# GpSimd splits each weight unit in six instructions instead of two

## The reference

```python
def first_block(x, ...):      # hybrid layer
    proj = rms_norm(x, norm_pre_w) @ w_in                 # 1024 -> 4104
    a = moba_attention(q, k, v) * silu(a_z)               # 8 heads of 64
    qkv = silu(causal_depthwise_conv(concat(d_q, d_k, d_v), conv_w))
    g = gated_delta_rule(qkv, g, beta)                    # 4 heads of 128
    mixed = concat(a, rms_norm(g) * silu(d_z)) @ w_out
    return x + rms_norm(mixed, norm_post_w)

def second_block(x, ...):
    proj = rmsnorm(h, norm1_g) @ w_in
    y_a = hgrn2_mixer(...)                                # 4 heads of 128
    y_b = nsa_mixer(...)              # compressed, selected and window attention
    merged = sigmoid(g_a) * (y_a @ w_br_a) + sigmoid(g_b) * (y_b @ w_br_b)
    h = h + merged @ w_out
    h = h + square(relu(rmsnorm(h, norm2_g) @ w_ff1)) @ w_ff2   # 1024 -> 4096 -> 1024
    return rmsnorm(h, final_g)
```

## Time and profile before

| | |
|---|---|
| median of 3 runs | 1343.54 us (1341.25 to 1349.25) |
| profiled execution | 1340.13 us, span 1338.1 us |
| TensorE busy | 1246.7 us, 93% |
| VectorE busy | 642.6 us, 48% |
| GpSimd busy | 580.2 us, 43% |
| ScalarE busy | 317.1 us, 24% |
| mean granted TensorE clock | 0.969 of full speed |

### The profile page before, as it was taken

How to read it: one execution, slowest core, us unless ns; L and a number is a source line. 1 busy time by engine, 2 the same in 40 slices (tenths; PEclk the granted TensorE clock), 3 DMA queues, 4 the chain that set the end, 5 groups by cost and what they waited for, 6 DMA issues and landing times.

```text
span 1338.1 us, 17644 instructions
## 1 busy us (share of the span) xinstructions
PE 1246.7 (93%) x6326; PEld 1034.9 (77%) x6326; DVE 642.6 (48%) x1189; ACT 317.1 (24%) x639; POOL 580.2 (43%) x332
## 2 busy tenths in 40 slices
PE   7898899998799799999997999998999999999996
PEld 6676688887688677788786888876888888888885
DVE  3974546548472478563735444457153500153202
ACT  3114221121472123311213344431031200021001
POOL 5543323322104456454420333334666666666662
PEclk9998999999899899999977999999999999999998
DMA  6211111100101222223420111112223232222321
GB/s 234 95 63 47 48 33 47 47 32 31 48 1 48 86 78 95 64 79 111 150 79 17 48 48 48 48 51 77 82 92 97 98 104 94 95 94 94 115 89 63
DMA packets 28870, 99.29 MB, mean 74 GB/s; under 512 B 3472, under 2 KB 5904, under 8 KB 28176
## 3 DMA queue, kind: packets, MB, share of 16 engines
q1 hardware_dynamic: 26592, 91.60, 20.7%
q10 hardware_dynamic: 2224, 6.94, 1.5%
HBM read 95.39 MB, written 2.10 MB: 73 GB/s over the span
## 4 chain that ended last, share of the span: by engine, by line
PE 55%; DVE 3%; issue 1%; ACT 0%; DVEq 0%; ACTq 0%
PE acc L266 15%; PE acc L268 15%; PE acc L267 15%; PE aux L449 3%; PE aux L467 2%; PE aux L716 2%; PE aux L457 1%; PE aux L745 0%; PE aux L641 0%; PE aux L328 0%; DVE mt_lo L1238 0%; DVE merged_b L1246 0%; PE aux L761 0%; DVE k_padded L1125 0%; DVE normalized L1288 0%
## 5 line engine op out<-in xcount | busy, mean ns | idle before, releaser
L1338 POOL CAST w_hi<-w_raw 128x1024 fp32r<-128x1024 f32 x164 | 175.0, 1067 | 724.7 <-issue 530.3
L1340 POOL TENSOR_TENSOR w_lo<-w_raw,w_hi 128x1024 fp32r<-128x1024 f32 x164 | 405.0, 2470 | 13.2
L266 PE MATMUL acc<-ht_hi,w_hi 128*128 128x512 f32 x672 | 283.5, 422 | 9.3 <-DVE feature_major L1588 5.1
L268 PE MATMUL acc<-ht_hi,w_lo 128*128 128x512 f32 x672 | 265.6, 395 | 0.0
L267 PE MATMUL acc<-ht_lo,w_hi 128*128 128x512 f32 x672 | 265.1, 394 | 0.0
L266 PEld LDWEIGHTS acc<-ht_hi,w_hi 128*128 128x128 f32 x672 | 128.9, 192 | 40.7 <-issue 8.9
L267 PEld LDWEIGHTS acc<-ht_lo,w_hi 128*128 128x128 f32 x672 | 128.9, 192 | 30.3 <-issue 4.3
L268 PEld LDWEIGHTS acc<-ht_hi,w_lo 128*128 128x128 f32 x672 | 128.0, 190 | 28.0
L266 PE MATMUL acc<-w_hi,ht_hi 128*128 128x512 f32 x256 | 106.4, 416 | 0.3 <-DVE feature_major L1009 0.3
L268 PE MATMUL acc<-w_hi,ht_lo 128*128 128x512 f32 x256 | 101.3, 396 | 0.0
L267 PE MATMUL acc<-w_lo,ht_hi 128*128 128x512 f32 x256 | 101.0, 395 | 0.0
(11 more groups left out here) (350 smaller groups left out, 1950.5 us busy)
## 6 DMA issues: line engine op xcount, KB each, us to landing
w_raw<-units SPq DMA_DIRECT2D x164, 512.0 KB, 3.3
cmp_w<-w_kv ACTq DMA_DIRECT2D x4, 1024.0 KB, 5.2
residual<-x SPq DMA_DIRECT2D x4, 512.0 KB, 6.9
result<-normalized SPq DMA_DIRECT2D x4, 512.0 KB, 2.8
consts_sb<-consts SPq DMA_DIRECT2D x1, 1344.5 KB, 11.4
norm_post_sb<-norm_post ACTq DMA_DIRECT2D x1, 512.0 KB, 4.7
cmp_tokens<-feature_major ACTq DMA_DIRECT2D x4, 128.0 KB, 2.9
final_sb<-final_g ACTq DMA_DIRECT2D x1, 512.0 KB, 3.3
```

The source lines that it names most:

```text
L266: nc.tensor.matmul(bank, ah, bh, start=start, stop=False)
L268: return nc.tensor.matmul(bank, al, bh, start=False, stop=stop)
L1338: nc.gpsimd.tensor_copy(w_hi[:, slot], raw[:, j]).then_inc(hi_split, 1)
L1340: nc.gpsimd.tensor_tensor(w_lo[:, slot], raw[:, j], w_hi[:, slot].bitcast(F32), ALU.subtract).then_inc(w_split, 1)
```

## The change

Each unit is split by six instructions instead of two. The cast becomes two of 128x512, one for each block of rows, and the subtraction four of 128x256, half a block each. The semaphores hi_split and w_split are raised once per unit, by the last of the two and of the four. The waits of all engines stay as they are.

```diff
                 slot = j % PARTS
-                nc.gpsimd.tensor_copy(w_hi[:, slot], raw[:, j]).then_inc(hi_split, 1)
+                for kk in range(2):
+                    done = nc.gpsimd.tensor_copy(w_hi[:, slot, kk], raw[:, j, kk])
+                done.then_inc(hi_split, 1)
                 pool.wait_ge(hi_split, unit + 1)
-                nc.gpsimd.tensor_tensor(w_lo[:, slot], raw[:, j], w_hi[:, slot].bitcast(F32),
-                                        ALU.subtract).then_inc(w_split, 1)
+                for kk in range(2):
+                    for first in (0, NC // 2):
+                        cols = slice(first, first + NC // 2)
+                        done = nc.gpsimd.tensor_tensor(w_lo[:, slot, kk, cols], raw[:, j, kk, cols],
+                                                       w_hi[:, slot, kk, cols].bitcast(F32), ALU.subtract)
+                done.then_inc(w_split, 1)
```

## The result

| | before | after |
|---|---|---|
| median | 1342.39 us (4 runs, 1338.27 to 1349.25) | 1322.19 us (4 runs, 1320.62 to 1329.17) |
| profiled execution, span | 1340.13, 1338.1 | 1321.77, 1320.0 |
| VectorE busy | 642.6 | 589.3 |
| GpSimd busy | 580.2 | 726.5 |
| mean granted clock | 0.969 | 0.980 |

The account below looks back on a forecast made before the run. TensorE was taken as the bound, stopped by any split over 4.76 us. Terms of 12 + 4.4 + 0.5 - 2 - 7.4 - 1.4 gave +6.1 us: 1346.2 profiled, about 1350 as median, range 1326 to 1370.

Parts of the forecast that it names:

- The bound and the cushion: TensorE bounds the kernel at 5.44 us per unit; a GpSimd split, then 3.51, has 1.25 spare, so 4.76 stops TensorE.
- The price of a seam: Each GpSimd unit: a lone split takes 3.9 us; a dense one, with VectorE entering at five seams, 6.15.
- the tiles: Delta-rule tiles: four TensorE waits of 1.85 us for gdn_U go, -7.4 us.
- the feed-forward: First product, eight slabs: a dense unit costs TensorE 1.4 us each, the unit before 0.1; together +12 us.
- the compressed keys: Units 70 to 72: the forecast said nothing of them; change put at 0.
- units 45 to 54: 495 to 538 us: dense units put TensorE 5.4 us back, against a shorter ScalarE wait and 1.7 of clock; +0.5 us.
- the convolution: 38 to 105 us: VectorE's 16 instructions finish at 58, but GpSimd falls behind; TensorE reaches the bank at 62.3; -2 us.
- the merge: 904 to 936 us: two waits on merged_b, 3.4 us, go; two tight units lose 1.0 each; -1.4 us.
- VectorE passes cheaply and the gains win: Rival, chance 0.18: a pass costs GpSimd only 0.33 us; -10 to -15 us, 1325 to 1333.
- GpSimd did not become the bound: Rival, with dense units much worse, 0.17: pieces cost over 0.3 us each beyond their share, tightly fed units lose; 1360 to 1380.
- the burst did not stay whole: Rival, chance 0.2: GpSimd's pieces follow directly, VectorE gets in nowhere new; 0 to +6 us, 1340 to 1350.
- The chains of tiny instructions: VectorE's rsqrt steps at 24, 476 and 655 us: six blocked about 0.6 each instead of two at 0.8 and 2.1; 0.

Follow-up runs that it names:

- tiles-only kernel: The kernel before, with six instructions only for units 16 to 31, the delta-rule tiles; 1330.44 us, ratio 0.9933.
- feed-forward-only kernel: The kernel before, with six instructions only for the feed-forward's 64 units (100 to 163), two for the first 100; 1354.97 us, ratio 1.007.
- casts-only kernel: The kernel before, with the cast in two of 128x512 and the subtraction whole in every unit; 1326.11 us, ratio 0.9868.
- keys-only experiment: The kernel before, with six instructions only for units 68 to 71, just ahead of the compressed keys; 1336.73 us, ratio 0.9981.

## Why the prediction was wrong

**The bound and the cushion** held. TensorE starts 0.05 us after the end of w_lo (976.87 to 976.92) where 0.13 had been allowed, so the limit was 4.84 and not 4.76.

**The price of a seam** was nearly right: a lone split 4.06 against 3.9, a dense one 6.24 against 6.15. VectorE does get in at seams without a semaphore; no VectorE instruction of the tiles or the feed-forward takes more than 1.23 us, so none is held longer than one piece. The feed-forward cost 10.5 against 12, the heads 2.7 against 4.4. (By the estimate in the prediction from the Trainium skill, GPSIMD Engine Reference, Performance versus the Vector engine, a fixed 0.29 us per instruction, the lone split would be 3.51 + 4 x 0.29 = 4.67, where the prediction wrote 4.5 to 4.6; the trace shows 4.06.)

**Where it failed is on the side of the gains**, and in one stall. Forecast and profiled change are 24.2 us apart (+6.1 and -18.1): 8.8 in the compressed keys, 4.0 in units 45 to 54, 3.3 in the convolution, 3.1 in the tiles, 1.7 in the heads, 1.6 in the merge and 1.5 in the feed-forward.

*Stalls that did not come.* The step said that two dense units at 1.3 and two at 1.4 put TensorE 5.4 back ahead of unit 52, and let that eat the 4.2 us wait. Units 45 to 50 changed by 0.7, 0.2, -0.3, -0.1, 0.4 and 0.1: 1.0 in all. To stall TensorE by 1.4, a unit needs five VectorE instructions ready one behind the other; I had taken that for four units from the way VectorE was held before. The splits of units 46, 47, 50 and 51 took 5.80, 5.68, 5.49 and 5.15 us, none 6.15, and before had lost 0.5 in unit 47 itself. Nor does the second of two such units in a row pay its excess over 4.84. The split of unit 47 began at 484.86, as soon as that of unit 46 was done, and TensorE needed 5.63 from unit to unit: it lost 0.19, the excess over its own 5.44. That is the mis-sized number. The rest of the step, a shorter wait and the clock kept, was right and unopposed: -4.6, and -3.5 for the stage where +0.5 had been written.

*The convolution* was given 1.2 us per VectorE instruction, 19 us for 16, and GpSimd behind at 62.3. It took 16.7 (38.80 to 55.48), 1.04 each, and TensorE reached the bank at 61.7. So TensorE gained 3.3 up to there, counted from its first unit, and not 2.3. The text names the full clock behind the wait, but prices it nowhere and lets the next three units take "it" back. It was 2.64 us (unit 8 took 8.49, then 5.85), and the units behind took back 0.6 and 0.9. Not all of it is the change's: in three of four kernels with before's program here unit 8 took 6.9 to 7.1. -5.3 against -2.

*The tiles* were credited with the wait for gdn_U alone, 1.85. The instructions behind it (L1668 of before) are caught less long too; 2.2 in each of the four stages up to unit 30 and 1.7 in the one behind. -10.5 against -7.4. *The merge* likewise, -3.0 against -1.4.

*The compressed keys* were put at nothing under the small chains. The profile of before had a wait of 2.98 us and 15.5 us at a clock of 0.54 there, more clock lost than anywhere else in the kernel, and no step of the prediction looked at it. Of the 18.1 us between the two spans, 8.8 come from here: 0.7 is the wait, 5.6 the clock of the 64 matmuls (13.00 against 7.36), and the rest lies in the matmuls around them. Some of the 8.8 is the scatter of single executions. Three of the four kernels with before's program in this stage took 3.2 to 3.3 less than before did, most of it because 32 matmuls a little further on (L745) took 3.79 to 4.61 us there and 6.42 in before. Against those three the changed kernel's stage is 5.5 shorter. Whether that rest is the change's doing stays open, as below; the ratio of 0.985 holds it in most executions.

Without the keys the stages add to about -9, so the sign would have been missed in any case, by the first three terms. The rival that ended on the right side ("VectorE passes cheaply and the gains win") had a wrong mechanism: a pass costs 0.44, not 0.33, and the feed-forward paid in full. What it had right was that the gains and the clock behind them outweigh the price. GpSimd did not become the bound, and the burst did not stay whole.

**The chains of tiny instructions** came out even, as said: six of them take 0.52 to 0.67 instead of two that take 0.96 and 2.25. But they show one way in which a whole subtraction can cost time in one execution and not in another. In before's profile the four instructions of L397 behind the chain are held little; in an execution of the tiles-only kernel, with whole splits at this place, one of them stood behind a subtraction, and TensorE waited 2.3 us longer:

```profile
481.01 1.91 DVE L397 TENSOR_SCALAR rstd_diagonal<-consts_sb,small 128x128 f32<-128x128 f32 x4
483.06 1.10 PE L359 MATMUL aux<-rstd_diagonal,consts_sb 128*128 128x512 f32 x2 [1.53 <-DVE rstd_diagonal L397]
```

```profile
470.58 4.23 DVE L397 TENSOR_SCALAR rstd_diagonal<-consts_sb,small 128x128 f32<-128x128 f32 x4
474.95 2.05 PE L359 MATMUL aux<-rstd_diagonal,consts_sb 128*128 128x512 f32 x2 [3.86 <-DVE rstd_diagonal L397]
```

The stage, units 34 to 45, then took 80.2 us instead of 75.7. The same happened in both places in the feed-forward-only kernel (37.7 against 33.2 at its start, units 0 to 5, and 80.3 here). In the profiles of the six kernels with split subtractions at these places the four instructions take 1.98 us at the most; that is seen, not proved, since it is one execution each. Nor does a whole subtraction make a kernel scatter by itself: the four executions of the casts-only kernel lie within 1.9 us.

## What to carry to other kernels

Where VectorE and GpSimd exclude each other, the length of one GpSimd instruction is the longest that VectorE can be made to wait, and each seam costs what it lets through: here 0.14 us for the piece and 0.44 for the pass. Cut the instructions where VectorE is on the path that TensorE waits for, and leave them whole where the fed engine has less slack than the dense split takes. The first cut, one more seam, brings most of the gain. When such a change is priced, count for a stalled unit only the instructions that are really ready, and for the second of two stalled units only what exceeds the fed engine's own time. Take the clock behind each wait into the sum: here it was about as large as the waits, and it scattered between executions by itself. So compare a stage with several executions of the old program before a gain in it is credited.

## What the runs showed of the hardware that was not expected

- A waiting VectorE instruction gets in between two GpSimd instructions that follow one another without a semaphore, at every seam: five times in a unit of 6.24 us. (The Trainium skill, SBUF — State Buffer, Who interferes with whom, has the exclusion for a whole instruction; the trace agrees, with no VectorE instruction of the feed-forward over 1.23 us beside pieces of 0.74.)
- A VectorE instruction on four columns is held in the same way: beside GpSimd's pieces it takes 0.52 to 0.67 us where it takes 0.16 alone.
- The granted clock behind one and the same wait of 2.27 us, after the same instructions, was 1.00 in two profiled executions and 0.51 in a third that reached the place 1.0 and 2.1 us later than they did. Before the wait all three ran at full clock. What decides it isn't settled: neither the wait's length nor the pieces just ahead of it, as the keys-only experiment shows; a shift of the whole program by a few us was not tried.
